# Attention of a hybrid encoder on one core: dense products dealt to other steps of a pair

## What is computed

```python
def chunk_attention(h, w_qkv, rel_bias, w_out):     # 16 heads of 64, CHUNK = 64, LEFT_CHUNKS = 8
    qkv = (h @ w_qkv).reshape(bsz, seq, 3, N_HEADS, HEAD_DIM)
    ...
    def one_chunk(c):                               # 64 queries see their own chunk and 8 before it
        s = jnp.einsum('bqhd,bkhd->bhqk', qc, kc).astype(jnp.float32) * scale + bias
        s = jnp.where(valid[None, None], s, -jnp.inf)
        p = jax.nn.softmax(s, axis=-1).astype(vc.dtype)
        return jnp.einsum('bhqk,bkhd->bqhd', p, vc)
    ...
    return o @ w_out
```

## Time and profile before

| | us |
|---|---|
| median of 3 runs | 2761.05 |
| the profiled execution, as a run | 2762.53 |
| its span, first to last instruction | 2760.7 |
| PE busy | 2621.3 (95%) |
| DVE, ACT, Pool busy | 1266.8, 654.3, 799.4 |
| PE waiting for the row maximum (line 1203) before scores | 25.4 |
| PE waiting for the low part (line 1211) before transposes | 16.9 |
| mean granted clock of TensorE, 1 is full speed | 0.985 |

### The profile page before, as it was taken

How to read it: one execution, slowest core, us unless ns; L and a number is a source line. 1 busy time by engine, 2 the same in 40 slices (tenths; PEclk the granted TensorE clock), 3 DMA queues, 4 the chain that set the end, 5 groups by cost and what they waited for, 6 DMA issues and landing times.

```text
span 2760.7 us, 33357 instructions
## 1 busy us (share of the span) xinstructions
PE 2621.3 (95%) x12148; PEld 2157.7 (78%) x12148; DVE 1266.8 (46%) x2092; ACT 654.3 (24%) x1219; POOL 799.4 (29%) x450
## 2 busy tenths in 40 slices
PE   6999999999999999999879999999789999999997
PEld 5878888877888888888667777777668888888885
DVE  7225555566222222222856556556773333222225
ACT  3112111122000000000455555555630000000002
POOL 3223322233333333333212221122133333333335
PEclk9999999999999999999989999999999999999998
DMA  4223211111111111111100110111011111111101
GB/s 138 97 88 111 72 59 59 65 41 51 46 53 53 46 46 46 46 46 46 40 33 31 40 36 23 38 40 40 24 46 54 46 46 46 46 53 53 46 31 61
DMA packets 53221, 143.50 MB, mean 52 GB/s; under 512 B 5392, under 2 KB 15776, under 8 KB 53168
## 3 DMA queue, kind: packets, MB, share of 16 engines
q1 hardware_dynamic: 35632, 119.71, 12.7%
q10 hardware_dynamic: 17536, 23.07, 2.5%
HBM read 130.13 MB, written 12.63 MB: 52 GB/s over the span
## 4 chain that ended last, share of the span: by engine, by line
PE 87%; DVE 9%; ACT 2%; issue 2%; DMA 0%; DVEq 0%; SPq 0%; ACTq 0%
PE bank L442 18%; PE bank L444 18%; PE bank L443 18%; PE scores L442 4%; PE scores L443 4%; PE scores L444 4%; PE probs_t L444 4%; PE probs_t L443 4%; PE probs_t L442 4%; PE probs_t L607 2%; DVE full L968 2%; DVE prob L1203 1%; PE scores L598 1%; PE bank L630 1%; PE bank L629 1%
## 5 line engine op out<-in xcount | busy, mean ns | idle before, releaser
L442 PE MATMUL bank<-hn_hi,w_hi 128*128 128x512 f32 x2048 | 811.9, 396 | 28.2 <-DVE hn_lo L973 23.8
L444 PE MATMUL bank<-hn_hi,w_lo 128*128 128x512 f32 x2048 | 802.1, 392 | 0.0
L443 PE MATMUL bank<-hn_lo,w_hi 128*128 128x512 f32 x2048 | 801.1, 391 | 0.0
L360 POOL TENSOR_SCALAR w_hi<-raw 128x1024 fp32r<-128x1024 f32 x212 | 247.3, 1167 | 1897.4 <-PE bank L444 1322.4
L362 POOL TENSOR_TENSOR w_lo<-raw,w_hi 128x1024 fp32r<-128x1024 f32 x212 | 519.7, 2451 | 17.7
L442 PEld LDWEIGHTS bank<-hn_hi,w_hi 128*128 128x128 f32 x2048 | 386.9, 189 | 112.7 <-DVE hn_lo L973 18.2
L444 PEld LDWEIGHTS bank<-hn_hi,w_lo 128*128 128x128 f32 x2048 | 386.5, 189 | 82.2
L443 PEld LDWEIGHTS bank<-hn_lo,w_hi 128*128 128x128 f32 x2048 | 387.0, 189 | 77.8 <-issue 1.2
L1043 DVE TENSOR_TENSOR full<-bank,atmp 128x512 f32<-128x512 f32 x88 | 60.9, 692 | 715.7 <-ACT atmp L821 714.1
L821 ACT ACTIVATE atmp<-bank 128x512 f32<-128x512 f32 x88 | 52.6, 598 | 1152.4 <-PE bank L444 1152.4
L1052 DVE TENSOR_TENSOR x<-probs_t,x 128x512 f32<-128x512 f32 x240 | 162.7, 687 | 110.5 <-PE probs_t L444 110.3
(11 more groups left out here) (138 smaller groups left out, 3593.3 us busy)
## 6 DMA issues: line engine op xcount, KB each, us to landing
raw<-w_units_in SPq DMA_DIRECT2D x212, 512.0 KB, 3.2
v_raw<-v_scratch ACTq DMA_DIRECT2D x16, 512.0 KB, 4.0
bias<-rel_scratch ACTq DMA_DIRECT2D x8, 640.0 KB, 3.7
x<-x_t_in SPq DMA_DIRECT2D x16, 256.0 KB, 6.5
v_scratch<-atmp ACTq DMA_DIRECT2D x16, 256.0 KB, 2.5
v_scratch<-full ACTq DMA_DIRECT2D x16, 256.0 KB, 2.7
out_t<-x SPq DMA_DIRECT2D x16, 256.0 KB, 2.0
ws_raw<-w_s_t_in ACTq DMA_DIRECT2D x8, 64.0 KB, 1.8
```

The lines of the kernel that those rows point to most:

```text
L360: pool.tensor_scalar(w_hi[slot][:, :], raw[r][:, :], 1.0, 1.0, ALU.mult, ALU.mult).then_inc(w_split, 1)
L442: pe.matmul(out, lh, rh, start=start, stop=False)
L443: pe.matmul(out, lh, rl, start=False, stop=False)
L444: last = pe.matmul(out, ll, rh, start=False, stop=stop)
```

## The change

The tables deal the same groups otherwise. `OUT1P` is spread from steps 3 to 7 over steps 3 to 9 and 11, one a step. The first half of the next queries starts in step 4 and not 8, with one group in most steps to 12 and its last group in step 15 and not 14. `OUT0` has two groups in step 16 and ends in step 18; the last pair keeps the old table under the name `OUT0_LAST`. The second half of the next queries starts in step 17 and not 16. Both parts of the query copy stand in step 15 and not 14; in DVE's program that is behind step 15's maximum and low part. `order` follows: the queries' first half ends behind three output groups and not two.

```diff
-                order[pair] += out_events("out0", 0, 2) + [(("q", 0), 2)] + out_events("out0", 2, KT) + [(("q", 1), 2)]
+                order[pair] += out_events("out0", 0, 3) + [(("q", 0), 2)] + out_events("out0", 3, KT) + [(("q", 1), 2)]
...
-        OUT1P = {3: (0, 1), 4: (2,), 5: (3, 4), 6: (5,), 7: (6, 7)}
-        OUT0 = {13: (0, 1), 14: (2,), 15: (3,), 16: (4,), 17: (5,), 18: (6,), 19: (7,)}
-        NEXT_Q = [{8: (0,), 9: (1, 2), 11: (3, 4), 13: (5, 6), 14: (7,)}, {16: (0,), 17: (1, 2), 18: (3, 4), 19: (5,)}]
+        OUT1P = {3: (0,), 4: (1,), 5: (2,), 6: (3,), 7: (4,), 8: (5,), 9: (6,), 11: (7,)}
+        OUT0 = {13: (0, 1), 14: (2,), 15: (3,), 16: (4, 5), 17: (6,), 18: (7,)}
+        OUT0_LAST = {13: (0, 1), 14: (2,), 15: (3,), 16: (4,), 17: (5,), 18: (6,), 19: (7,)}
+        NEXT_Q = [{4: (0,), 5: (1,), 6: (2,), 7: (3,), 9: (4,), 10: (5,), 12: (6,), 15: (7,)}, {17: (0, 1), 18: (2, 3), 19: (4, 5)}]
...
-                    for n in OUT0.get(m, ()):
+                    for n in (OUT0_LAST if last else OUT0).get(m, ()):
...
-                    if m == 14 and not last:
+                    if m == 15 and not last:
                         query_hi(it, 0)
...
-                    if m == 14 and not last:
+                    if m == 15 and not last:
                         query_lo(it, 0)
```

## The result

The changed kernel takes 2766.14 us (median of 18 runs, 2763.48 to 2769.16), the kernel before 2761.14 (18 runs, 2760.03 to 2763.48): a ratio of 1.0018, 95% interval 1.001 to 1.0025. That is 5 us slower, just inside the 0.2% that the prediction calls no change, and 18 from its forecast of 2748.0.

What follows compares the result with a forecast made beforehand. PE was taken to bound each pair of heads except in its waits. Six middle pairs -6.8, first pair -3.85 and last -2.5 summed to -13.1 us, from the median 2761.05 to 2748.0; range 2743 to 2756.

Steps and rivals of the forecast that it cites:

- weight splits: Pool's output-weight split, now after step 11: ready 4.0 after step 12's scores start, wanted at 6.1, so no cost.
- T14: Start of transposes of step 14's probabilities, run in step 17: 17.75 after step 12's scores start, against 18.51 before.
- rival 1: Clock falls once in each middle pair, in step 13 or 16, at the new waits: 2756; chance 0.12.
- T13: Start of transposes of step 13's probabilities, run in step 16: its wait of 1.64 was to go.
- S3 to S9: Middle pair, start of step 3's scores to step 9's: one group more, +0.11, plus at most 0.1 for a new wait.
- S9 to S12: Middle pair, start of step 9's scores to step 12's: step 10's group hidden in idle, step 11 loses one, -0.69.
- First and last pair: First pair of heads: -3.85 in all; last pair: -2.5, with step 13 -1.6 if its clock is kept.
- The rest -0.2: First pair's remainder, beside -2.05 up to step 9's scores and -1.6 for steps 9 and 11.
- Rival 2: Groups in steps 10 and 12 delay transposes or maximum, costing as elsewhere: +1.4 per middle pair, about 2757; chance 0.10.
- Rival 3: Query copy in step 15 delays step 14's transposes by its whole 2.55: +18, clock +5, about 2769; chance 0.06.
- Rival 4: Better: clock drops at the 1.64 waits go as well and the chain is kinder: 2744; chance 0.10.

Runs made afterwards that it cites:

- held kernel: The changed kernel with Pool made to wait for o_lo of step 12 before splitting the next keys' weights, likewise after the last pair: 2746.47 us, ratio 0.9946.
- one with even steps: The held kernel with two query groups moved from steps 5 and 7 to steps 8 and 10: 2737.49 us, ratio 0.9916.
- run with the old output groups: The changed kernel with the OUT1P table of before, the previous pair's output groups all done by step 7: 2750.6 us, ratio 0.996.
- run with one SBUF operand: The changed kernel with o_lo made as a scaled copy of o_full instead of the subtraction, its value left out: 2765.58 us, ratio 1.0013.

## Why the prediction was wrong

**The step that failed** is the one on the weight splits: "ready 4.0 after S12. Step 13 wants it at 6.1, so nothing, with 2.1 to spare", and with it, in S9 to T14, o_lo "ready at 5.98 ... doesn't move". The splits' delay was seen, and weighed only against PE, the reader of the split weights. What DVE does while Pool splits wasn't asked. Pool's next split, that of the keys, lies from 4.0 to 7.4 after S12, and o_lo of 0.69 was due at 5.3. o_lo was ready 8.0 after S12 and the output group started 8.1 after it, not 6.1 (1656.90 less S12 at 1648.79):

```profile
1648.79 0.34 PE L599 MATMUL scores<-k_hi,q 128*128 128x384 f32 x1
```

That is +2.0 in six middle pairs and +1.9 in the last; not in the first, where no output groups stand in front of Pool's split (o_lo 0.69). The held kernel shows what the change is worth without it: 15.35 us faster than before, where the prediction had 13.1.

**The clock, rival 1.** It falls in five middle pairs, at step 13, behind the wait of 1.93. But several short idles did not bring it, as that rival had it: the held kernel and the one with even steps, with idles of 0.35 to 0.8 in the same places, have no fall in a middle pair. It came behind the one long wait that the meeting made, as it had behind T13's 1.64 in the first and the fifth pair of the kernel before. Its price was 1.2 to 1.5, against the 1.05 in the prediction. First and last pair kept their clock in the places named: 1.00 in the first pair's steps 4 to 8 and in the last pair's step 13.

**Point by point**, for the pair without the meeting:

| Step | predicted | measured |
|---|---|---|
| S3 to S9, against before | +0.2 | -0.25 |
| S9 to S12 | -0.69 | -0.31 |
| S12 to S14 | 7.55 | 7.60 |
| S14 to S15 | 2.54 | 2.36 |
| T13, after S15 | 4.35 | 4.40 |
| T14, after S15 | 7.65 | 7.50 |
| wait for bank 1 in step 16 | 1.05 | 0.77 |
| T14 to the next pair, against before | +0.1 | 0.0 |
| middle pair | 75.4 | 75.0 |
| first pair, against before | -3.85 | -5.1 (held), -5.5 (changed) |
| last pair, S0 to S15 (held) | -2.5 | -2.7 |

The shortfall of S9 to S12 is in step 9, which is 3.90 where it was left at its old 3.50. Its two groups were both queries in front of the values; now one is an output group behind them. On DVE, the add of step 8's new output group comes ahead of o_full, and the values start just behind o_full's end, 2.16 after S9 (changed kernel, fourth pair; S9 at 1639.55):

```profile
1640.20 0.68 DVE L1152 TENSOR_TENSOR x<-bank,x 128x512 f32<-128x512 f32 x1
1640.80 0.87 DVE L1172 TENSOR_TENSOR o_full<-bank,o_side 64x256 f32<-64x256 f32 x2
```

```profile
1641.71 0.39 PE L630 MATMUL bank<-pt_hi,v 128*128 128x256 f32 x1
```

In the run with the old output groups, step 8 has none and the values start 1.93 after S9. That is 0.23 of the 0.4; the rest stays open. S3 to S9 came out better because the output group taken from step 3 gave back 0.69 in full, while the two added cost 0.42 together where the sum had 0.80. In the first pair, steps 4 to 8 went from 12.36 to 10.37, about the -2.05 that was forecast. The term mis-sized is "The rest -0.2": S15 to the next pair went from 36.03 to 34.68 and step 13 from 5.77 to 5.11. T12 to the next pair had been 1.0 longer there than in a middle pair, as in the fifth pair, whose clock fell (0.72 from 1440 to 1446 us in the first pair); behind the shorter waits it no longer is.

**Rival 2** (groups in steps 10 and 12 not hidden): wrong; steps 10 and 12 are 2.26 and 2.41 with a group, 2.30 and 2.41 without. **Rival 3** (the copy): wrong in its mechanism, though it alone ended on this side of before; T14 is where it was forecast. It was also added up wrongly: 2748 and 18 and 5 make 2771, not 2769. **Rival 4**: both falls of the clock behind 1.64 are gone in the held kernel and its chain is kinder, as that rival had it, but at 2746.5 it stays short of the 2744.

The sum of the result, from medians: 2761.8 before, less 15.35 of what the change does, is 2746.5. The changed kernel is 19.7 above that (2766.14 less 2746.47). The pairs account for 20.8: the meeting 2.0 in six of them and 1.9 in the last, 13.9; five falls of the clock, 7.2 (four of 1.5, one of 1.2); less 0.3, by which its first pair is shorter than the held kernel's. The 1.1 between is no more than the profiled executions stand from their medians. Those executions are only 16.5 apart: in the changed kernel's, attention happens to start 3.7 earlier (1389.49 against 1393.18).

The held kernel's 15.35 is less than its pairs gave, too. The six middle pairs gained 10.7, the first 5.1, the last 2.7 up to S15, 18.5 in all, against 15.6 between the two profiled executions (2760.7 and 2745.1). Attention starts 1.5 later in the held one, and from the last pair's S15 to the end it takes 1.4 longer. The sum had put both at nothing; their cause stays open. That the 13.1 lies so near the 15.35 is in part luck.

## What to carry to other kernels

Where a change moves the release of an engine's work, ask not only who needs that work but what runs beside it in its new place. Here Pool's splits, which read SBUF, held the DVE subtractions with both operands in SBUF until shortly after their own end, and the scaled copy of 128x512 too. In the trace of before this shows as instruction groups whose longest is two to three times their median (o_lo, h_lo); look at those before taking a duration as fixed. A product moved to a step that another engine bounds cost 0.2 to 0.3 here instead of 0.7; at least one in every step is not the aim.

## What the runs showed of the hardware

- A DVE subtraction or scaled copy of 128x512 from SBUF alone that starts during Pool's split ends 0.3 to 0.6 after Pool's instruction, not a full duration after it: 2.69 and 2.83 for the subtraction beside a w_lo and 1.45 beside a w_hi (0.69 free), 2.42 for the scaled copy beside a w_lo (0.43 free).
- It goes the other way as well. Pool's w_hi that followed at 1656.32, while o_lo still ran to 1656.78, took 1.36 instead of 1.05. In the trace of before, the w_lo at 1685.94, under step 19's o_lo, took 2.72 instead of 2.38.
- The trace doesn't name the holder: PE's wait is put down to o_lo on DVE in six pairs and, in the last, to Pool's w_lo, and o_lo's own row shows a long duration with no wait in front of it.
- TensorE's granted clock went to the lower of its two levels behind one idle of 1.93 us in a stretch otherwise busy, in five of six middle pairs, and as often behind the 1.67 of the run with one SBUF operand. Behind T13's 1.64 in the kernel before it fell in one of six. It stayed up behind the 1.69 in the last pair's step 13, and behind the idles of up to 0.8 in the held kernel's middle pairs.
